# Attention body blocks of a two-layer decoder on Trainium2: softmax steps handled in pairs, transposes and scores placed together

## The reference, cut to what matters

```
GROUPS = ((128, 1), (512, 4), (2048, 16))          # window, dilation; 16 heads of 64 each
q = rmsnorm(x, norm_g) @ w_q                       # 3 groups x 16 heads x 64
k, v = rmsnorm(x, kv_norm_g) @ w_kv                # shared, same shape each
for each group g:
    s = q k^T * 64**-0.5 + bias[g]                 # only keys of the group's window and stride
    m = max(s); p = exp(s - m); l = sum(p)
    o_g = p v / l;  lse_g = m + log(l)
out = sum_g softmax_g(lse)[g] * o_g                # merged per head
x = x + out @ w_out
```

## Time and profile before

| | before |
|---|---|
| timed runs, us | 761.25, 762.6, 764.22 (median 762.6) |
| the profiled execution's own time, us | 762.83 |
| its span, first to last instruction, us | 761.1 |
| TensorE busy | 747.7 us (98%) |
| VectorE busy | 537.9 us (71%) |
| ScalarE busy | 458.4 us (60%) |
| GpSimd busy | 228.4 us (30%) |
| mean granted TensorE clock | 0.994 |
| DMA | 136.24 MB, mean 179 GB/s |

### The profile page before, as it was taken

The page is one execution under the profiler, slowest core; times in us unless marked ns, Lnnn a source line. Parts: engine busy times, 40 slices in busy tenths (PEclk is TensorE's granted clock), DMA queues, the critical chain, the costliest instruction groups (busy, mean ns, idle before and its releaser), DMA issues.

```text
span 761.1 us, 16940 instructions
## 1 busy us (share of the span) xinstructions
PE 747.7 (98%) x6428; PEld 736.2 (97%) x6428; DVE 537.9 (71%) x998; ACT 458.4 (60%) x610; POOL 228.4 (30%) x187
## 2 busy tenths in 40 slices
PE   8999999999999999999999999999999999999995
PEld 8999999999999999999999999999999999999994
DVE  6875877888888465557746756756788888887452
ACT  7744567656565556358547647746867566655451
POOL 2251346322223422312322322320214222233321
PEclk9999999999999999999999999999999999999998
DMA  9674265565654665844664384384545656454731
GB/s 281 189 217 158 88 225 179 184 213 184 201 171 153 206 194 192 273 139 133 195 223 145 108 264 138 110 256 143 171 161 173 211 176 220 166 186 142 238 98 55
DMA packets 140301, 136.24 MB, mean 179 GB/s; under 512 B 3825, under 2 KB 139329, under 8 KB 140260
## 3 DMA queue, kind: packets, MB, share of 16 engines
q1 hardware_dynamic: 129620, 130.43, 52.8%
q10 hardware_dynamic: 10640, 5.25, 2.7%
HBM read 134.54 MB, written 1.13 MB: 178 GB/s over the span
## 4 chain that ended last, share of the span: by engine, by line
PE 93%; DVE 3%; ACT 1%; issue 1%; DMA 1%; POOL 0%; POOLq 0%; SPq 0%; DVEq 0%
PE bank L1403 16%; PE bank L1405 15%; PE bank L1404 15%; PE banks L1403 9%; PE banks L1405 9%; PE banks L1404 9%; PE bank L1637 3%; PE bank L1639 3%; PE bank L1638 3%; PE banks L1671 2%; PE banks L1682 2%; PE bank L1437 1%; PE bank L1439 1%; PE bank L1438 1%; PE banks L1714 1%
## 5 line engine op out<-in xcount | busy, mean ns | idle before, releaser
L483 POOL TENSOR_TENSOR wlo<-raw,whi 128x512 fp32r<-128x512 f32 x162 | 214.8, 1358 | 480.9 <-ACT whi L530 480.9
L530 ACT ACTIVATE whi<-raw 128x2048 fp32r<-128x2048 f32 (+2 forms) x135 | 236.5, 1752 | 179.3 <-PE bank L1405 91.4
L898 DVE TENSOR_TENSOR wlo<-raw,whi 128x1024 fp32r<-128x1024 f32 x162 | 198.0, 1259 | 7.1 <-ACT whi L530 6.5
L1403 PE MATMUL bank<-xsA,whi 128*128 128x256 f32 x552 | 154.7, 280 | 2.4 <-DVE wlo L975 2.4
L1405 PE MATMUL bank<-xsA,wlo 128*128 128x256 f32 x552 | 153.2, 278 | 0.0
L1404 PE MATMUL bank<-xsA,whi 128*128 128x256 f32 x552 | 153.2, 278 | 0.0
L1403 PE MATMUL bank<-xsB,whi 128*128 128x256 f32 x480 | 134.2, 280 | 0.3 <-DVE wlo L898 0.2
L1405 PE MATMUL bank<-xsB,wlo 128*128 128x256 f32 x480 | 132.6, 276 | 0.0
L1404 PE MATMUL bank<-xsB,whi 128*128 128x256 f32 x480 | 132.6, 276 | 0.0
L1403 PEld LDWEIGHTS bank<-xsA,whi 128*128 128x128 f32 x552 | 104.3, 189 | 3.0 <-DVE xsA L918 2.6
L1404 PEld LDWEIGHTS bank<-xsA,whi 128*128 128x128 f32 x552 | 104.5, 189 | 0.1
(11 more groups left out here) (200 smaller groups left out, 1541.5 us busy)
## 6 DMA issues: line engine op xcount, KB each, us to landing
raw<-in_f_w_up SPq DMA_DIRECT2D x44, 1024.0 KB, 5.1
raw<-in_w_kv SPq DMA_DIRECT2D x24, 1024.0 KB, 6.5
raw<-in_f_w_down SPq DMA_DIRECT2D x16, 1024.0 KB, 5.2
raw<-in_b_w_q SPq DMA_DIRECT2D x12, 1024.0 KB, 5.2
raw<-in_a_w_in SPq DMA_DIRECT2D x10, 1024.0 KB, 5.5
raw<-in_f_w_down SPq DMA_DIRECT2D x8, 768.0 KB, 4.8
Bi<-bias_by_distance ACTq DMA_DIRECT2D x16, 320.0 KB, 4.7
raw<-in_a_w_out SPq DMA_DIRECT2D x4, 1024.0 KB, 5.4
```

The lines of the kernel that those rows point to most:

```text
L483: o = g.tensor_tensor(wlo[s][:, ka:kb, :], raw[s][:, ka * CW:kb * CW] .rearrange("p (k c) -> p k c", c=CW), whi[s][:, ka:kb, :].bitcast(F3 ...
L530: o = a.activation(whi[s][:, k0:k1, :], raw[s][:, k0 * CW:k1 * CW] .rearrange("p (k c) -> p k c", c=CW), ACT.Copy)
L898: v.tensor_tensor(wlo[s][:, ka:kb, :], raw[s][:, ka * CW:kb * CW].rearrange("p (k c) -> p k c", c=CW), whi[s][:, ka:kb, :].bitcast(F32), A ...
L1403: t_.matmul(ps, hi_w, hi_x, start=first, stop=False)
```

## The change

Only the three looped blocks are reordered; the number of instructions of each kind stays the same. The fourth block keeps its order. The core of the diff:

```diff
@@ ScalarE, block @@
                 for j in range(4):
                     hi(n0 + j + 3, i, step)
+                if not last:
+                    for t in range(4):
+                        if t:
+                            p_hi(2 * t - 2)
+                            p_hi(2 * t - 1)
+                        soft(2 * t)
+                        if t:
+                            v_hi(3 + t, 1)
+                        soft(2 * t + 1)
+                        normed(2 * t)
+                        normed(2 * t + 1)
+                        if t == 1:
+                            load_bias(2)
+                            load_bias(3)
+                        if t < 3:
+                            v_hi(4 + t, 0)
+                        hi(n0 + 7 + t, i, step)
+                    a_cross(0)
+                    a_cross(1)
+                    p_hi(6)
+                    p_hi(7)
+                    a_hi(0)
+                    a_hi(1)
+                    hi(n0 + 8 + 3, i, step)
...
+                    return
@@ VectorE, block @@
+                if not last:
+                    for t in range(4):
+                        if t:
+                            p_lo(2 * t - 2)
+                        biased(2 * t)
+                        biased(2 * t + 1)
+                        inverse(2 * t)
+                        if t:
+                            p_lo(2 * t - 1)
+                        inverse(2 * t + 1)
+                        if t:
+                            evac(3 + t, 1)
+                        if t < 3:
+                            lo(n0 + 6 + t, i, step, 0, KD // 2)
+                        evac(4 + t, 0)
+                        if t < 3:
+                            lo(n0 + 6 + t, i, step, KD // 2, KD)
+                    evac(7, 1)
+                    a_sum(0)
+                    a_sum(1)
+                    p_lo(6)
+                    p_lo(7)
...
+                    return
@@ TensorE, block @@
+                if not last:
+                    def both_steps(t):
+                        if t:
+                            turned(2 * t - 2)
+                            turned(2 * t - 1)
+                        if t < 4:
+                            scores(t)
+                    for t in range(4):
+                        tile(4 + t, 0, lambda: both_steps(t))
+                        if t < 3:
+                            tile(4 + t, 1)
+                    tile(7, 1)
+                    mixed(0)
+                    tile(8, 0, lambda: both_steps(4))
+                    tile(8, 1)
+                    mixed(1)
+                    return
```

More of the change, by code:

```diff
@@ L834, in block @@
                     hi(n0 + j + 3, i, step)
+                if not last:
[22 more added lines that the diff above has]
+                    hi(n0 + 8 + 3, i, step)
+                    a_cross(2)
+                    a_cross(3)
+                    a_hi(2)
+                    a_hi(3)
+                    return
                 soft(0)
@@ L839, in block @@
                     normed(m)
-                    if last and m == 6:
+                    if m == 6:
                         a_cross(0)
@@ L846, in block @@
                     p_hi(m)
-                    if m and not (last and m > 4):
+                    if 0 < m < 5:
                         h0 = (m + 1) % 2 * (KD // 2)
@@ L851, in block @@
                 normed(7)
-                if not last:
-                    hi(n0 + 7 + 3, i, step)
-                    a_cross(0)
                 a_cross(1)
@@ L857, in block @@
                 a_hi(0)
-                if last:
-                    hi(n0 + 9)
+                hi(n0 + 9)
                 a_hi(1)
-                if not last:
-                    hi(n0 + 8 + 3, i, step)
                 a_cross(2)
@@ L1319, in block @@
                     evac(j, 1)
+                if not last:
[20 more added lines that the diff above has]
+                    p_lo(7)
+                    a_lo(0)
+                    a_lo(1)
+                    lo(n0 + 9, i, step)
+                    evac(8, 0)
+                    evac(8, 1)
+                    a_sum(2)
+                    a_sum(3)
+                    a_lo(2)
+                    a_lo(3)
+                    return
                 biased(0)
@@ L1745, in block @@
                         scores(m // 2 + 1)
[L1746 to L1756, removed]
+                turned(5)
+                projected(0, 2)
+                mixed(0, lambda: turned(6))
+                projected(2, HEAD_K, lambda: turned(7))
                 mixed(1)
```

## The result

The change makes the kernel slower. The median of five timed runs is 773.25 us (772.11 to 774.12) against 761.62 us of before (761.25 to 764.22); the ratio is 1.0144, 95% interval 1.0129 to 1.0159. The profiled execution took 774.12 us. Executions of one kernel fall into groups about 1.5 us apart (the kernel before: near 761.3 and near 763.0), so the median of the kernel before is 761.62 here and 762.75 to 762.99 beside the experiments.

A forecast was written before the change was run, and what follows sets the result against it. TensorE's own order, plus a microsecond of waits, was taken to bound the time between 300 and 560 us. -0.7 + 0 + 0 + 0.4 = -0.3 on 762.83 gave 762.5, so 762.4 for the timed median; range 759.9 to 766.0.

The forecast's parts named there:

- part 4: Bias loads of heads 2 and 3, now behind normed(3): landing 0.3 and 0.8 us late, +0.4 us in all.
- Rival 1: Late bias holds VectorE at biased(5), then TensorE before tile(7, 0): 767.3 us, or 771.6 with a landing of 8.4; chance 0.14.
- The rule: DMA engines alternate packets between rings: head 3's bias would land 6.1 instead of 5.5 us after issue, time 764.3 us.
- Part 1: Grouping on TensorE: scores behind transposes start 0.21 us later, as behind a tile matmul; nothing won or lost, 0.
- Rival 3: Grouping saves because scores enter free behind transposes on TensorE: -2.4 and -0.7, giving 759.7 us; chance 0.10.
- Part 2: TensorE's wait at the first transposes of the three blocks goes away: -0.7 us.
- Part 3: Read-out evac(3 + t, 1) behind both inverse on VectorE: in time for its half tile with 0.4 us spare, 0.
- Rival 2: Read-out on VectorE comes short at nine places, from a path 0.6 us longer than summed: 765.3 us; chance 0.12.

The follow-up runs named there:

- one_level: The changed kernel with head 2's bias load behind soft(2) and head 3's behind normed(3), held to leave in the same moment as the weight load: 765.04 us.
- experiment 1: The changed kernel with head 2's bias load moved right behind soft(2) and head 3's right behind soft(3), ahead of both normed: 761.84 us.
- experiment 6: The kernel before, unpaired and ungrouped, with both bias loads moved behind normed(3) in all four blocks: 788.12 us.
- one_later: The changed kernel with head 2's bias load behind soft(2) and head 3's behind v_hi(5, 0): 761.87 us.

## Why the prediction was wrong

**The wrong step** is in part 4, "for the second of the pair I add the first's share ... so 320 KB are 1.0 us. ... head 3 at 407.0 + 5.5 = 412.5, 0.8 late". The landing was not 5.5 but 9.4, 7.6 and 8.0 us, so that TensorE waited 3.64, 1.85 and 2.28 us instead of 0.1; head 3's late bias, the place of the wait and its followers were as described. (Head 2's was not 0.3 late but just in time.) Two errors make the term. The base, 4.5 us, came from a load issued 1.14 us ahead of its weight load; level with it, `one_level` shows 6.3 to 6.6. And the price of 320 KB was taken from the weight load of the same pair of rows, which met only the rest of a bias load: by that trace's packets, over three quarters of its bytes had moved when the first bytes of the weight load did. That gave 6.2 instead of 5.2. In `one_level` one whole bias load makes the weight load land at 6.6 to 7.0, 1.4 to 1.8 later, and in the change the two make it 7.7 to 9.5. I had written that the load leaves "in the same moment", and then took a row in which it did not. The range had an upper end of 766.0 because of this size.

**Rival 1** is what happened, near its bound of 8.4: I had 9.5 us of waits for it and it was 7.8, mainly since the loads left 0.4 us sooner than I had summed. Its 771.6 comes near the measured time partly by luck, since it lacks the 4.4 us of clock. I gave it 0.14. The rows for pairs beside weight loads, 6.2 to 7.0 and up to 8.4, spoke for it and were the nearer ones: same size, both queues busy. The nearest row of all I had passed over. In the kernel before, ahead of the first block, the second load of a pair leaves level with a weight load, as in the change:

```profile
L784 ACTq DMA_DIRECT2D Bi<-bias_by_distance x1: 943/943/943, 309.5 to 309.5; - x1
...
DMA to landing us min/median/max: 8.1/8.1/8.1
```

```profile
L363 SPq DMA_DIRECT2D raw<-in_w_kv x1: 372/372/372, 309.4 to 309.4; - x1
...
DMA to landing us min/median/max: 7.5/7.5/7.5
```

My argument against rival 1, that two weight loads had been ahead in those cases, does not hold for this one. By rival 1's own working a landing of 8.1 gives about 770.5 us.

**The clock** was in no part of the prediction: a wait on TensorE stood in the sum at its own length plus a fresh start. 4.4 us of the 11.3 come from it. Before, no wait in these blocks was longer than 0.3 us, so nothing in the trace hinted at the price of a long one, but a rival with waits of 3 us on TensorE should have named the granted clock.

**The rule** of the Trainium skill (DMA: Bandwidth & Descriptors, section Queues, rings and completion order), taking turns by packets between the rings, pointed the right way: by it I had 6.1 us (how 6.1 follows from the 5.5 and the 2.0 us was not worked out there). The runs agree in that both loads land together (9.4 and 9.5) and that each delays the other. Packets by queue show the turns; q1 is SyncE's with the weights, q10 ScalarE's with the bias. The kernel after, 349 to 350 us, and the kernel before, 404 to 405, where a bias load runs alone (packets, MB, share of the engines):

```profile
q1 hardware_dynamic: 242, 0.25, 70.2%
q10 hardware_dynamic: 239, 0.12, 40.5%
```

```profile
q10 hardware_dynamic: 395, 0.20, 75.4%
```

Both queues move as many packets, and as the bias load's are half as large, it moves half the bytes, at 239 packets a microsecond instead of the 395 that it moves alone. It is not so all the time: from 347 to 348 us of the kernel after it was 262 packets to 110. The size of 6.1 us was not borne out, for two reasons. I had worked it out with the same 1.0 us for 320 KB, and I had counted equal turns as equal bytes, 640 KB of the weight load. In turns by packets the pair's 1280 packets have the whole weight load, 1024 packets, between them: by my own price 3.2 us instead of 2.0, an estimate of 7.3 instead of 6.1, and near the 7.6 of the second block.

**Part 1, grouping, 0:** right. The second block of the kernel after:

```profile
406.56 0.28 PE L1694 MATMUL bank<-whi,xsA 128*128 128x256 f32 x1
406.68 1.03 PE L1737 MATMUL banks<-ident,SB 128*128 128x128 f32 x8
407.65 1.15 PE L1726 MATMUL banks<-KT,QT 64*128 64x256 f32 x12
408.72 0.39 PE L1692 MATMUL bank<-whi,xsA 128*128 128x256 f32 x1
408.95 0.28 PE L1693 MATMUL bank<-wlo,xsA 128*128 128x256 f32 x1
```

The whole group adds 408.95 - 406.56 - 0.24 = 2.15 us, and the same pieces apart 2 x 0.44 + 1.27 = 2.15. The scores start 407.65 - 406.68 - 7 x 0.11 = 0.20 us behind the last transpose, as behind a tile matmul. Rival 3 fell.

**Part 2, -0.7:** right. No wait at the first transposes of the three blocks; the blocks of experiment 1 are 0.17, 0.34 and 0.36 us shorter than before, 0.87 in all.

**Part 3, the read-out with 0.4 spare:** right, and on the safe side. In experiment 1 no half tile waits for it; its `evac(5, 1)` of the first block ends at 351.28 + 0.48 = 351.76, and `tile(7, 0)` begins at 352.59, so 0.8 us is spare. At the block's two other places it is 0.8 and 0.7. Rival 2 fell.

## What to carry to other kernels

A DMA issue is an instruction like any other: when an order is rewritten, list the issues that it moves, and for each the transfer on the other queue that will leave in the same microsecond. A transfer's time beside another must be read from a row in which both leave together; a row in which one had a microsecond's lead gave 4.5 us for what took 6.3 to 6.6 level and 7.6 to 9.4 as the second of a pair. And a wait of some microseconds on TensorE is not priced by its length: add what the granted clock does after it.

## What the runs showed of the hardware

- A 320 KB bias load and a 1 MB weight load on the two queues, 3.2 to 3.7 and about 5.2 us alone, both land 6.3 to 7.0 us after a common issue, and with a second bias load just ahead 7.6 to 9.5. A lead of 0.5 to 0.6 us brings the bias load's landing back to 4.7 to 5.7.
- While a bias load ran alone the DMA engines moved fewer bytes for the time they were busy than while weight loads ran. The kernel before, windows of 1 us (last two: DMA share, GB/s):

```profile
404.00:405.00 1.00, 1.00 (x11) 1.00 (x10) 1.00 (x3) 1.00 (x2) 0.00 (x0) 1.00 0.75 197
```

```profile
373.00:374.00 1.00, 1.00 (x12) 1.00 (x11) 0.86 (x3) 0.47 (x2) 0.00 (x0) 1.00 1.04 370
```

  Per byte the bias load thus took 1.4 times the engines' time (0.75/197 against 1.04/370). Why the bias load gets less than its turns in the first microseconds of a common transfer was not tried.
- TensorE's clock after idle stretches (idle time as the trace gives it): in the kernel after, 3.5 us idle and then 1.2 GHz for 6.8 us, begun during the idle stretch, 2.7 us of loss; 2.1 us idle and then 3.4 us, begun 1.1 us after it, 1.7 us of loss. In the kernel of experiment 6, 5.8 us idle was followed by 6.8 us of the low clock, but three idle stretches of 3.9 to 4.4 us by 3.4 us each. So how long the low clock lasts does not follow the length of the last idle stretch. An idle stretch of 1.7 us kept the clock full and one of 1.8 did not; whether length or something else parts these two stays open.
- ScalarE's queue sent a DMA up to 0.65 us before the instruction ahead of it in the program began (`one_later`, 345.23 against 345.88).
